# Attention: which half of a head's probabilities TensorE transposes first

## What is computed

```python
sc = jnp.einsum('bgrqd,bgkd->bgrqk', qi, k_all).astype(jnp.float32) * scale
p = jax.nn.softmax(sc, axis=-1).astype(v_all.dtype)
return jnp.einsum('bgrqk,bgkd->bgrqd', p, v_all)
```

## Time and profile before

| | |
|---|---|
| median of 3 runs | 1719.2 us (1719.05 to 1720.28) |
| profiled execution, its own time | 1719.3 us |
| its span, first to last instruction | 1717.6 us |
| TensorE matmuls busy | 1657.2 us, 96% |
| VectorE busy | 1006.1 us, 59% |
| ScalarE busy | 637.0 us, 37% |
| GpSimd busy | 233.4 us, 14% |
| mean granted TensorE clock | 0.992 of full speed |

### The profile page before, as it was taken

One profiled execution on the slowest core, in us unless ns is written; L12 is line 12 of the kernel. 1 busy time (PEld: TensorE's weight loads), 2 busy tenths in 40 slices (PEclk: granted clock), 3 DMA queues, 4 the chain that ended last, 5 costly groups with the idle time before them and its releaser, 6 DMA issues.

```text
span 1717.6 us, 26527 instructions
## 1 busy us (share of the span) xinstructions
PE 1657.2 (96%) x9828; PEld 1334.1 (78%) x9828; DVE 1006.1 (59%) x1912; ACT 637.0 (37%) x1123; POOL 233.4 (14%) x378
## 2 busy tenths in 40 slices
PE   6999899999999999999999999998999999999998
PEld 2877566668898888888878878886678888888886
DVE  4655566754747777777776496315753744443445
ACT  3414555653421212121324443225543533333343
POOL 0413233330100000000000023204420100000000
PEclk9999999999999999999999999998999999999999
DMA  8687231266513353434334454323404443332243
GB/s 318 191 275 220 81 91 35 45 89 213 179 50 99 98 147 98 140 105 130 114 101 146 140 183 140 121 88 55 123 16 135 124 122 98 96 95 66 86 135 135
DMA packets 242584, 211.36 MB, mean 123 GB/s; under 512 B 54201, under 2 KB 204601, under 8 KB 242489
## 3 DMA queue, kind: packets, MB, share of 16 engines
q1 hardware_dynamic: 236186, 199.28, 39.0%
q0 software_dynamic: 4288, 9.10, 1.4%
q10 hardware_dynamic: 2016, 1.73, 0.4%
HBM read 186.58 MB, written 23.48 MB: 122 GB/s over the span
## 4 chain that ended last, share of the span: by engine, by line
PE 86%; DVE 5%; ACT 4%; DMA 2%; issue 2%; SPq 1%; POOL 1%; ACTq 0%; DVEq 0%
PE ps L1361 31%; PE ps L889 10%; PE ps L891 10%; PE ps L890 10%; PE ps L1126 4%; PE ps L1237 4%; PE ps L1032 3%; PE ps L1184 3%; PE ps L1371 2%; PE ps L1175 1%; PE ps L1347 1%; PE ps L1346 1%; PE ps L1345 1%; ACT arena L1727 1%; PE ps L946 1%
## 5 line engine op out<-in xcount | busy, mean ns | idle before, releaser
L1903 DVE TENSOR_TENSOR w_lo<-w_raw,w_hi 128x2048 fp32r<-128x2048 f32 (+3 forms) x112 | 204.0, 1822 | 244.0 <-ACT w_hi L1510 243.3
L889 PE MATMUL ps<-w_hi,act_hi 128*128 128x512 f32 (+2 forms) x872 | 337.6, 387 | 2.6 <-DVE act_lo L1903 1.4
L890 PE MATMUL ps<-w_lo,act_hi 128*128 128x512 f32 (+2 forms) x872 | 333.0, 382 | 0.0
L891 PE MATMUL ps<-w_hi,act_lo 128*128 128x512 f32 (+2 forms) x872 | 332.9, 382 | 0.0
L1361 PE MATMUL ps<-act_lo,w_hi 128*128 128x512 f32 (+1 forms) x912 | 277.8, 359 | 0.0
L1361 PE MATMUL ps<-act_hi,w_hi 128*128 128x512 f32 (+1 forms) x912 | 276.2, 357 | 0.0
L1361 PE MATMUL ps<-act_hi,w_lo 128*128 128x512 f32 (+1 forms) x912 | 274.3, 355 | 0.0
L1510 ACT ACTIVATE w_hi<-w_raw 128x2048 fp32r<-128x2048 f32 (+2 forms) x106 | 166.1, 1567 | 270.0 <-PE ps L891 211.9
L889 PEld LDWEIGHTS ps<-w_hi,act_hi 128*128 128x128 f32 x872 | 164.2, 188 | 39.5 <-issue 9.3
L891 PEld LDWEIGHTS ps<-w_hi,act_lo 128*128 128x128 f32 x872 | 164.2, 188 | 30.8
L890 PEld LDWEIGHTS ps<-w_lo,act_hi 128*128 128x128 f32 x872 | 164.4, 189 | 29.3
(11 more groups left out here) (157 smaller groups left out, 2098.4 us busy)
## 6 DMA issues: line engine op xcount, KB each, us to landing
arena<-in_ada_w SPq DMA_DIRECT2D x44, 1024.0 KB, 8.2
w_raw<-in_ffn_up SPq DMA_DIRECT2D x88, 512.0 KB, 5.2
w_raw<-in_ffn_down SPq DMA_DIRECT2D x88, 256.0 KB, 3.0
w_raw<-in_odd_w_in SPq DMA_DIRECT2D x20, 512.0 KB, 4.5
arena<-mods SPq DMA_DIRECT2D x16, 512.0 KB, 7.0
x_after_mix<-arena SPq DMA_DIRECT2D x10, 512.0 KB, 3.0
arena<-x_after_mix SPq DMA_DIRECT2D x10, 512.0 KB, 6.3
wide_raw<-in_ada_w SPq DMA_DIRECT2D x4, 1024.0 KB, 13.8
```

The costliest lines, as they stand in the source:

```text
L889: mm(out_, s_hi, m_hi, start=start, stop=False)
L890: mm(out_, s_hi, m_lo, start=False, stop=False)
L891: return mm(out_, s_lo, m_hi, start=False, stop=stop)
L1903: V.tensor_sub(out_, full, hi.bitcast(fp32)).then_inc(sem_, 1)
```

## The change

`turns` gets a flag, and `probs_t`, which transposes a head's probabilities, sets it: the right group (bank 7, copied by VectorE) now comes first and the left group (bank 6, copied by ScalarE) second. `prep`, which calls the same function, keeps left first. No instruction is added or removed, and the instructions of the other four engines and their waits are the same, in the same order.

```diff
-                def turns(r, left, right):
-
-                    for srcs, b, done, free in ((left, 6, left_done, left_free), (right, 7, right_done, right_free)):
+                def turns(r, left, right, vector_first=False):
+
+                    groups = [(left, 6, left_done, left_free), (right, 7, right_done, right_free)]
+                    for srcs, b, done, free in groups[::-1] if vector_first else groups:
                         at_least(pe, free, R0 + r)
...
-                    turns(a.unit_round[k, x], srcs[:(n + 1) // 2], srcs[(n + 1) // 2:])
+                    turns(a.unit_round[k, x], srcs[:(n + 1) // 2], srcs[(n + 1) // 2:], True)
```

## The result

The changed kernel took **1725.3 us** (median of 8 runs, 1723.5 to 1726.3) where the kernel before, on the same chip and at the same time, took 1720.3 (median of 8 runs, 1718.0 to 1723.3). The ratio is 1.0034, with a 95% interval of 1.0025 to 1.0044: slower, by more than the 0.2% that a measurement of this kernel can tell from no change. The prediction said 1727.5, in a range from 1722.6 to 1731; its change was 8.3 us from 1719.2, the measured one is 5.0 us.

A forecast was written before the change was run, and what follows sets the result against it. The prediction took TensorE to bound the kernel, with order and waits counting in attention. Terms of 2.8, 1.7, 2.0 and 1.8 summed to 8.3 us over 1719.2, stated as 1727.5 us, range 1722.6 to 1731.

The forecast's parts named there:

- the likeliest case: The forecast itself: the kernel gets slower, 1725 to 1731 us, chance 0.64.
- part b: In `mla` and `swa`, left transposes that filled a wait for VectorE now follow it: 1.3 and 0.4, sum 1.7 us.
- part c: In `na` and `swa`, a later left copy delays exponential, reciprocal, minima and scores in a loop: 2.0 and 1.8 us.
- The unit of 0.105 us: In the transposes, the left half is ready about 0.105 us later for each tile of the right half.
- Part a: At preps directly behind a head's second group, ScalarE's later copy delays TensorE: 0.11 to 0.32 each, 2.8 us.
- Only direct waits: Rival: in attention only preps' waits and formerly hidden transposes cost, loops have slack; 4.5 us, so 1723.8; chance 0.16.
- No change: Rival: the preps' delay in attention is made up; within 3.4 us of 1719.2; chance 0.08.
- faster: Rival: in `na` and `swa` VectorE's first-head copies move forward, and scores with them; about 1716 us; chance 0.04.
- The clock: Rival: new idles in attention bring some 7 us at half clock, about 3 us on top, 1730.6; chance 0.08.

The follow-up runs named there:

- first heads only: The changed kernel with right half first kept only for the first head of each step; 1724.2 us.
- second heads only: The changed kernel with right half first kept only for the second head of each step; 1728.0 us.
- the exponential moved ahead: ScalarE's second-head exponential queued before the left copy, in the changed kernel (1726.1 us) and in the kernel before (1726.3 us).
- the three sets: The changed kernel, without further edit, timed three times against the kernel before: 1725.3, 1723.6 and 1726.0 us.
- the run with six first heads: Against the kernel before, right half first in six first heads only, two in `mla` and one in each pair of `swa`; no time given.
- the copy among them: The kernel before, unchanged, timed against itself; 1718.7 us, ratio 0.9998.
- the kernel with preps alone: Against the kernel before, only the preps turn their right group first, every head keeps left first; 1720.3 us, ratio 1.0007.

## Why the prediction was right

**The mechanism** held in all three parts, and the forecast was the likeliest case: the kernel is slower, because ScalarE's half comes later by a tenth of a microsecond for each tile of the other half, and at the places counted ScalarE had no slack to make it up. That the sum of the terms, 8.3, lies so near the 7.8 of the ledger is in part luck: part b is too small by 0.4 us in `mla`, part c too large by 0.7 in `na`. The unit of 0.105 us is confirmed by the prep of the earlier trace rows, two tiles, 0.22 us.

**Part a (2.8 us) was sized right, within 0.1 us at each place looked at.** The idles at the two named preps grew by 0.10 and 0.22 (0.11 and 0.21 predicted). The two preps counted in `na` added 0.21 each (0.21 predicted), the long one in `mla` 0.25 (0.32), the two in `gqa` 0.25 and 0.33 (0.32 each). The first preps of the two stages, which were to cost nothing, added 0.14 in `na` and 0.32 in `gqa`; the latter comes with first heads only as well and not with second heads only.

**Part b (1.7 us) was too small in `mla`.** The two places that were run by themselves cost 0.39 each within the changed kernel, not 0.32, the remainder being the later start behind the copy where two conditions are waited for. The one that was to be absorbed, and to lengthen the next, shows 0.11 and 0.06 in two steps, and the next one cost 0.72. Before:

```profile
210.78 1.18 DVE L2175 TENSOR_TENSOR w_lo<-w_raw,w_hi 128x512 fp32r<-128x512 f32 x1 [0.35 <-ACT w_hi L1702]
210.87 1.29 PEld L1237 LDWEIGHTS ps<-arena 128*64 128x64 f32 x24 [0.17 <-issue]
...
212.32 0.31 PEld L1126 LDWEIGHTS ps<-ident,arena 128*128 128x128 f32 x3 [0.17 <-issue]
...
212.83 0.31 PEld L1126 LDWEIGHTS ps<-ident,arena 128*128 128x128 f32 x3 [0.19 <-DVE arena L2186]
```

After:

```profile
209.80 1.29 PEld L1238 LDWEIGHTS ps<-arena 128*64 128x64 f32 x24 [0.17 <-issue]
...
210.04 1.18 DVE L2176 TENSOR_TENSOR w_lo<-w_raw,w_hi 128x512 fp32r<-128x512 f32 x1 [0.36 <-ACT w_hi L1703]
...
212.15 0.64 PEld L1127 LDWEIGHTS ps<-ident,arena 128*128 128x128 f32 x6 [1.06 <-issue]
```

VectorE's weight split starts 0.24 us behind the context product where it started 0.09 ahead of it (0.33), the three left tiles come behind the wait (0.33), and the group starts 0.11 and not 0.05 behind the copy (0.06). The four places cost 1.67 us in sum and not 1.3.

**Part c (3.8 us) was sized too high in `na`.** The loop is there, as the exponential moved ahead shows. The term was 0.125 us a step over 16 steps; nine steps without a prep, at full clock, grew by 0.80, which is 0.09 a step, and the turn of the earlier trace rows by 0.05 in place of 0.2. With its two preps `na` lost 1.75 and not 2.4. In `swa` the term was 0.45 a pair; each of the two middle pairs loses 1.0 us, of which part a has 0.32 and part b 0.11 (0.17 as it was run by itself, with the bank asked for twice), so 0.51 to 0.57 is left for the loop, of which 0.36 is in the three steps that the exponential moved ahead frees. Over the stage, 3.03 us less 0.95 for part a and 0.51 for part b leaves 1.6 of the 1.8. The loop reaches TensorE through GpSimd as well, which the prediction had for `na` only. That `mla` and `gqa` absorb the loop is borne out: the steps of `mla` between its first ten and its last ones repeat to 0.01 us but for one prep of 0.11.

**The rivals.** Only direct waits: refuted by `na`'s steps without a prep, which grow, and by the 7.8 us. No change and faster: the three sets lie 5.0, 5.1 and 7.0 us above before, and their intervals begin at 1.0025, 1.0019 and 1.0030. That VectorE's earlier half could gain something (the case *faster*): its wait fell from 42.0 to 23.6 us, and the mechanism shows at one step, the first of `gqa`. There VectorE's copy and the second minimum behind it come earlier, and the step is 0.12 us shorter, in first heads only as in the changed kernel. It is far from the 4 us that this case needed.

**The clock** was not made worse by the change; see the next paragraph. The Trainium skill (TensorE: Matmul & The Clock Gate, section on a second HAM failure mode) had been set against the trace in the prediction. The 1.00 that the prediction names for attention does not stand in the earlier trace rows, which has 0.97 for the window with `mla` and 1.00 for the one between the attentions; read from behind the stretches at the start, 190 to 297 us and 1187.1 to 1303 us of the kernel before, the granted clock is 1.00. Nor are TensorE's idles there all under 1 us: one wait for a transfer in `na` took 1.09. No run shows swinging: in the changed kernel the window with `mla` is at 0.99 and steps behind the start are at full clock, though TensorE's idles ahead of the transposes had nearly doubled, up to 1.50 us. The one stretch at half clock in the midst of attention, in the run with six first heads, is told in the last section.

**Where the rest of the 7.8 us went.** Granted clock in the same windows (busy us of PE, PEld, DVE, ACT, POOL, then the clock) at the norm behind the second attention, kernel before:

```profile
1350.00:1355.00 5.00, 2.88 (x23) 2.68 (x23) 4.49 (x5) 1.37 (x3) 1.07 (x2) 0.93 1.05 278
1355.00:1360.00 5.00, 5.00 (x34) 5.00 (x34) 2.04 (x4) 0.89 (x2) 0.00 (x0) 0.72 0.67 162
```

The changed kernel, first profile:

```profile
1355.00:1360.00 5.00, 2.89 (x25) 2.69 (x24) 4.52 (x4) 1.38 (x4) 2.07 (x2) 1.00 1.06 290
1360.00:1365.00 5.00, 5.00 (x45) 5.00 (x44) 3.49 (x6) 2.05 (x4) 0.00 (x0) 1.00 0.91 219
```

The changed kernel, third profile:

```profile
1355.00:1360.00 5.00, 3.27 (x28) 3.07 (x26) 4.52 (x4) 2.42 (x6) 2.07 (x2) 1.00 0.91 267
1360.00:1365.00 5.00, 4.61 (x27) 4.61 (x28) 3.95 (x5) 1.08 (x2) 0.00 (x0) 0.67 1.18 287
```

TensorE is busy for 2.9 to 3.3 us of five each time, and behind that it is granted 0.72, 1.00 or 0.67. In the profile of before five us at 0.93 and five at 0.72 are 1.75 us of clock lost (0.35 and 1.4), in the first profile of the changed kernel nothing, in the third 1.65. What that is worth can be read from the starts of steps: from `gqa`'s last step to the end of the span it takes 433.1 us in each of the five profiles with this stretch, of whatever kernel, and 431.6 in each of the eight without. So the stretch costs 1.5 us, and nothing else behind attention differs between the kernels. Before's profile has one such stretch more at the start of `mla` as well, and the first profile of the changed kernel is 1.6 us ahead at step 3 (187.78 against 189.40). These two, with the 0.15 between `swa` and `na`, are the 3.3 us between the 7.8 of attention and the 4.5 of the span. The third profile of the changed kernel has as many us at half clock at each place as that of before, and its span is 7.2 us longer (1724.9 against 1717.6). Over all runs the mean granted clock is 0.9921 for the kernel before (73 runs, the copy among them) and 0.9925 for the changed one (23 runs); 0.001 of it goes with about 1.3 us of span (1719.9 us at 0.990, 1714.9 at 0.994 in the kernel before). Among runs at 0.992 the changed kernel is 6.7 us longer (1724.2 in 10 runs, 1717.5 in 28), among those at 0.993 5.5 us (1722.0 in 7, 1716.5 in 16). So the medians of 5.0 and 5.1 us were helped by fewer stretches at half clock, which the third set did not repeat.

**What stays open.** At equal clock 5.5 to 6.7 us are found, and the ledger says 7.8. The clock is given to 0.001 only, which is 1.3 us; whether that is all of the gap was not settled. Stretches are not all that spreads the runs either: a straight line through span and clock of the 73 runs of the kernel before, an estimate, takes up 60% of the variance. Nor was it settled what decides whether such a stretch comes: the kernel with preps alone had 0.9934 in 11 runs, those with one head changed 0.9908 in 8 and in 6, which is more apart than the sets of one kernel, so that the moment at which TensorE stands still may play a part.

## What to carry to other kernels

When two engines empty what TensorE fills, fill first for the one that has been waiting: its delay has nothing to be made up with, while the other's copy stands behind other work anyway. Which engine that is depends on the order of its queue: with the exponential ahead of the copy, the changed order was the cheaper one in `swa`. Look at the seams as well: an order that alternates the two banks across rounds gives each copy time to end, and turning over one kind of round alone can cost as much as turning over all. For changes worth a few tenths of a per cent compare the starts of like steps in two traces: they repeat to 0.01 to 0.03 us, where medians of eight runs differ by 1 to 2 us for reasons that have nothing to do with the change.

## What the runs showed of the hardware

In all 13 profiles there are stretches at half clock, from 3.4 to 10.2 us in sum at each place, at the same places: some 35 us into the kernel, at the start of `mla`, at the start of `na` and at the very end, and in five profiles at the norm behind the second attention as well, each time behind a spot at which TensorE was busy for only part of the time (1.13 us of 4 at the start of `na`, 2.9 of 5 at the norm). Their number differs between executions of one kernel. One execution, the run with six first heads, has such a stretch in the midst of `na` too, behind a transfer that came late there:

```profile
1229.12 0.44 PEld L1127 LDWEIGHTS ps<-ident,arena 128*128 128x128 f32 x4 [2.19 <-DMA arena<-proj_odd]
```

In the kernel before the same wait took 1.09 us and the clock stayed at 1.00. A stretch of 3.4 us costs 1.5 us at the norm and 1.7 at the start of `mla` (16.61 against 14.94 us from step 1 to step 3 in two profiles of the changed kernel); at the start of `na` 10.2 us cost 1.9 us more than 6.8 (19.21 against 17.35 us for its first four steps in the kernel before and its copy). Runs of the kernel before at a mean clock of 0.990 and at 0.994 differ by 5.0 us of span. Within attention, at full clock, the same kernel repeats its steps to 0.01 us from execution to execution (0.03 in `na`), across about 100 us with four engines waiting for one another. A group of transposes that waits for a copy starts 0.05 us behind the copy's end where its first instruction waits for one semaphore (221.36, 326.71, and 328.97 in the changed kernel), and 0.11 to 0.12 behind it where it waits for two, as the first group of a head does (221.19 in the changed kernel, 329.91, 330.42, 223.04 and 224.62 in the experiments). A prep of `mla` that waits for two starts 0.10 behind it (218.06 in the changed kernel), one of `swa` that waits for one 0.05 (328.97), so it goes with the number of waits rather than with what is transposed. No run changed that number by itself.
